# Where the filler matmuls of the projection sit between the steps of four attention heads

## The reference, cut to what matters

```
for l in range(DEPTH):                      # 2
    h = rms_norm(x, norm_mix_pre[l])
    z = h @ w_in[l]                         # one wide projection, split:
    q_h, f_fw, f_bw, i_h, g_h, q_d, k_d, v_d, gate_a, gate_b = split(z)
    a = hgrn2_mixer(q_h, f_fw, f_bw, i_h, g_h, ...)      # 4 heads, both directions
    b = diff_attention(q_d, k_d, v_d, ...)               # 4 heads
    m = sigmoid(gate_a) * (a @ w_branch_a[l]) + sigmoid(gate_b) * (b @ w_branch_b[l])
    x = x + rms_norm(m @ w_out[l], ...)
    x = x + rms_norm(conv_ffn(rms_norm(x, ...), ...), ...)
    x = x + rms_norm(sigmoid(rms_unit(x) @ w_ple_gate[l]) * (p[l] @ w_ple[l]), ...)
```

## The kernel before, in words

| head | 1 | 2 | 3 | 4 | 5 | 6 | 7 | 8 | 10 | 11 | 12 |
|---|---|---|---|---|---|---|---|---|---|---|---|
| second | 20,21 | 22,23 | 24 | 25,26 | 27,28 | 29,30 | 31 | 32 | 33 | 34,35 | 36 |
| third | 37,38 | 39,40 | 41,42 | 43,44 | 45,46 | 47,48 | 49 | 50 | 51,52 | 53 | 54 |
| fourth | 55,56 | 57,58 | 59 | 60,61 | 62,63 | 64,65 | 66 | 67 | 68 | 69,70 | 71 |

## Time and profile before

### The profile page before, as it was taken

One profiled execution on the slowest core, in us unless ns is written; L12 is line 12 of the kernel. 1 busy time (PEld: TensorE's weight loads), 2 busy tenths in 40 slices (PEclk: granted clock), 3 DMA queues, 4 the chain that ended last, 5 costly groups with the idle time before them and its releaser, 6 DMA issues.

```text
span 2431.4 us, 40402 instructions
## 1 busy us (share of the span) xinstructions
PE 2401.2 (99%) x16160; PEld 2235.7 (92%) x16160; DVE 1847.5 (76%) x2432; ACT 1314.8 (54%) x2035; POOL 191.1 (8%) x236
## 2 busy tenths in 40 slices
PE   9999999999999999999999999989999999999998
PEld 8999988898999999888889999888989999998887
DVE  7656887764888998978585578876648889999784
ACT  6445766543555556556454456664435555554563
POOL 1000111100200000003110011101002000000031
PEclk9999999999999999999999999999999999999999
DMA  5354444254323233833234544443543232346421
GB/s 185 127 177 144 134 140 142 99 179 148 104 72 101 83 101 111 297 119 124 97 130 133 182 132 147 137 134 101 180 148 102 75 89 83 105 159 251 150 98 61
DMA packets 287041, 320.97 MB, mean 132 GB/s; under 512 B 10500, under 2 KB 219400, under 8 KB 286856
## 3 DMA queue, kind: packets, MB, share of 16 engines
q1 hardware_dynamic: 213760, 171.39, 22.7%
q10 hardware_dynamic: 73096, 147.01, 16.6%
HBM read 253.08 MB, written 65.27 MB: 131 GB/s over the span
## 4 chain that ended last, share of the span: by engine, by line
PE 93%; DVE 3%; ACT 2%; issue 1%; DMA 0%; SPq 0%; ACTq 0%; DVEq 0%; POOLq 0%; POOL 0%
PE ps L911 23%; PE ps L1196 16%; PE ps L1396 13%; PE ps L1139 7%; PE ps L884 5%; PE ps L1502 5%; PE ps L1365 3%; PE ps L1332 3%; PE ps L898 3%; PE ps L1122 3%; PE ps L1260 3%; PE ps L1111 1%; PE ps L963 1%; PE ps L1091 1%; PE ps L1482 1%; PE ps L1020 1%
## 5 line engine op out<-in xcount | busy, mean ns | idle before, releaser
L2148 DVE TENSOR_TENSOR wlo<-raw,whi 128x1024 fp32r<-128x1024 f32 (+1 forms) x152 | 163.7, 1078 | 55.1 <-ACT whi L3174 55.1
L911 PE MATMUL ps<-hT_hi,whi 128*128 128x384 f32 x608 | 203.1, 334 | 0.0
L911 PE MATMUL ps<-hT_hi,wlo 128*128 128x384 f32 x608 | 203.1, 334 | 0.0
L911 PE MATMUL ps<-hT_lo,whi 128*128 128x384 f32 x608 | 203.1, 334 | 0.0
L3188 ACT ACTIVATE U<-ps 128x384 f32<-128x384 f32 x152 | 74.8, 492 | 223.9 <-PE ps L911 223.9
L1396 PE MATMUL ps<-whi,PH_hi 128*128 128x512 f32 x456 | 179.0, 393 | 0.0
L1396 PE MATMUL ps<-whi,PH_lo 128*128 128x512 f32 x456 | 177.7, 390 | 0.0
L1396 PE MATMUL ps<-wlo,PH_hi 128*128 128x512 f32 x456 | 177.5, 389 | 0.0
L1710 DVE TENSOR_TENSOR wlo<-raw,whi 128x1024 fp32r<-128x1024 f32 (+1 forms) x106 | 111.3, 1070 | 78.9 <-ACT whi L2645 78.8
L1583 DVE TENSOR_TENSOR wlo<-raw,whi 128x2048 fp32r<-128x2048 f32 x51 | 116.6, 2286 | 48.0 <-ACT whi L2469 48.0
L911 PE MATMUL ps<-S_hi,whi 128*128 128x384 f32 x456 | 152.3, 334 | 0.0
(11 more groups left out here) (349 smaller groups left out, 6968.5 us busy)
## 6 DMA issues: line engine op xcount, KB each, us to landing
raw<-w_up_dram SPq DMA_DIRECT2D x88, 512.0 KB
raw<-w_in_dram SPq DMA_DIRECT2D x66, 512.0 KB
raw<-w_down_dram SPq DMA_DIRECT2D x60, 512.0 KB, 4.6
zT<-gst ACTq DMA_DIRECT2D x40, 384.0 KB, 2.4
raw<-w_in_dram SPq DMA_DIRECT2D x14, 1024.0 KB
GT<-zT ACTq DMA_DIRECT2D x16, 768.0 KB, 5.8
zT<-hn ACTq DMA_DIRECT2D x52, 192.0 KB, 1.9
pD<-CG ACTq DMA_DIRECT2D x26, 384.0 KB, 2.3
```

The lines of the kernel that those rows point to most:

```text
L911: ins = mm(ps[:, 4 * (j % 2) + bank, 0:TH], quarter(L, W[y], j, (w,))[:, 0, k * P:(k + 1) * P], sum_operand(a, x, k), start=(opens and k = ...
L2148: v.tensor_tensor(lo, x, hi.bitcast(F32), ALU.subtract)\
```

## The change

Two numbers in the table of slots. The second head's slot 4 gets one part where it had two, and the fourth head's slot 3 gets two where it had one. The sum stays 72.

```diff
-SLOTS = ((2, 2, 2, 2, 2, 2, 2, 1, 1, 0, 2, 1, 1), (0, 2, 2, 1, 2, 2, 2, 1, 1, 0, 1, 2, 1),
-         (0, 2, 2, 2, 2, 2, 2, 1, 1, 0, 2, 1, 1), (0, 2, 2, 1, 2, 2, 2, 1, 1, 0, 1, 2, 1))
+SLOTS = ((2, 2, 2, 2, 2, 2, 2, 1, 1, 0, 2, 1, 1), (0, 2, 2, 1, 1, 2, 2, 1, 1, 0, 1, 2, 1),
+         (0, 2, 2, 2, 2, 2, 2, 1, 1, 0, 2, 1, 1), (0, 2, 2, 2, 2, 2, 2, 1, 1, 0, 1, 2, 1))
```

## The result

The changed kernel takes 2409.35 us (median of 4 runs, 2408.98 to 2409.67) where the kernel before took 2433.8 beside it. The ratio is 0.9901, 95% interval 0.9886 to 0.9916: 24.4 us faster. Forecast were 2409.9. The profiled execution took 2409.67 with a span of 2407.6.

What follows compares the result with a forecast made beforehand. TensorE, busy 2401.2 of 2431.4 us, bounds the kernel; only its waits can be won. Per layer 10.25 + 1.48 + 0.84 - 0.42 - 0.2 = 11.95, for two layers 23.9, giving 2409.9 us, range 2406.5 to 2417.

Steps and rivals of the forecast that it cites:

- The eight copy waits go: TensorE's waits for ScalarE's copy before parts 28 to 56 vanish: 7.85 listed plus 8 x 0.30, 10.25 us a layer.
- The far keys' wait: Third head, before line 1041: the 1.34 us wait goes as part 49 moves to slot 8; gain 1.48 a layer.
- Fourth head, slot 3: A second part there covers an At wait and one for attention weights in level 3; gain 0.84 us a layer.
- Second head, slot 4: Losing its second part, the slot leaves `att_values` waiting for the At copy; cost 0.42 us a layer.
- What gets tight: Part 51's copy and unit 22's low part in the fourth head's level 0 (margin 0.24); 0.2 us a layer together.
- The neighbour: Fourth head's level 0: GpSimd's running products could contend with unit 22's low part; no cost expected, up to 0.6 a layer.
- A: Unit 22's moved halves delay fourth-head weights and third-head x8t copy: 2418.3 us, halfway 2414; chance 0.18 at larger sizes.
- B: ScalarE's queue makes copies late, so each wait returns at the copy's new place: 2430 us; chance 0.05.
- C: Unit 24's load starts later, its lead shrinking from 56.8 to 29.3 us; ScalarE could stall, 2441 at 45 us; chance 0.03.
- D: Second head's slot 4 pays its whole lost cover, 2.05 instead of 0.42 a layer: 2413.2 us; inside the forecast's 0.72.

Runs made afterwards that it cites:

- e1: Against the kernel before: second head's slot 4 gets one part, third head's slot 1 three, so only parts 26 to 36 move; 2429.3 us, ratio 0.9984.
- e2: Against the kernel before: second head unchanged, third head's slot 1 gets one part, from part 38 on everything as in the changed kernel; 2415.14 us, ratio 0.9928.
- e3: Against the changed kernel: third head's slots 1 to 6 hold 1, 2, 2, 2, 2, 3 parts in place of six times 2; 2417.49 us, ratio 0.9935.
- e10: Kernel before with each copy of a gate unit's half cut to its first 384 of 768 columns; 2428.84 us, ratio 0.9982.
- e9: Kernel before with each copy of a gate unit's half preceded by one of its first 384 of 768 columns; 2444.79 us, ratio 1.0049.
- e4: Changed kernel with unit 22's high and low parts made at part 48 (third head's slot 7), not part 49; 2413.06 us, ratio 0.9917.
- e5: Kernel before with every copy of a gate unit's half out of banks 6 and 7 made twice; 2459.28 us, ratio 1.0104.
- e8: Changed kernel with two parts in the second head's slots 3 and 4, one in slot 11, none in slot 12; 2415.18 us, ratio 0.9926.

## Why the prediction was right

**The eight copy waits go, 10.25 a layer.** They went, all sixteen. Idle 15.7 to nothing, and the 0.30 beyond each held: slot 5 lost exactly 5.54 - 4.26. e1 and e2 show it in two parts, e3 puts two back at 0.98 each, and e10 and e9 show that what TensorE stood for was in the main the copy's own length. That ScalarE came late to four of the six copies of one form, by up to 0.6 us, is in the listed idle, so the sum had it without naming it.

**The far keys' wait, 1.48.** It went, and e4 shows by what: with unit 22's two halves one part earlier it is back. There it is worth 1.85 a layer by the medians and 1.74 by the listed waits, more than in the kernel before for the reason told above, so the term was right for the removal.

**Fourth head, slot 3, 0.84.** Both waits are missing from the changed kernel's table. No run took this step alone; it is in e2 and its 18.3.

**Second head, slot 4, -0.42.** One part from 329.28, `att_values` at 331.90: 2.62 against the 2.21 of a part alone, 0.41. The listed wait is 0.29.

**What gets tight, -0.2.** Not spent: neither place has a wait. The rows of the changed kernel, part 51's copy ahead of part 52, and the fourth head's level 1 behind unit 22's low part:

```profile
425.96 0.81 ACT L2598 ACTIVATE hn<-ps 128x768 f32<-128x768 f32 x1 [1.36 <-PE ps L1139]
...
426.97 0.61 PE L1139 MATMUL ps<-hT_hi,whi 128*128 128x384 f32 x2
...
436.30 2.29 DVE L1583 TENSOR_TENSOR wlo<-raw,whi 128x2048 fp32r<-128x2048 f32 x1
...
438.96 0.48 DVE L1842 SCALAR_TENSOR_TENSOR PR<-PR,lr 128x256 f32<-128x256 f32 x1
...
439.69 0.44 PE L1102 MATMUL ps<-ident,PR 128*128 128x128 f32 x2
```

The copy is over at 426.77, 0.20 early, and the weights at 439.44, 0.25 early; I had worked out 0.24. Without the 0.2 the sum is 24.3 for two layers. The heads gained 24.0, the two profiled spans differ by 23.8 and the medians by 24.4, so an agreement closer than some 0.5 us is luck. The neighbour, GpSimd's running products, ends at 435.84, 0.46 before the low part starts, and the low part takes its usual 2.29: no overlap came about, and no run here shows what one would cost.

**The rivals.** A needed the margin in the fourth head to be overrun, or a wait before line 1061 in the third, and there is neither. B, that the copies wait elsewhere, is refuted by ScalarE's waits in the changed kernel: before all 28 copies it is ScalarE that stands, and TensorE's part that it waits for (12 of 28 in the kernel before).

```profile
ACT hn L2598 <- PE ps L1139: 28.1, 14, 2.8
ACT gst L2598 <- PE ps L1139: 15.2, 14, 1.9
```

C, the load of unit 24, started at 438.68 in the changed kernel, 29.1 us before its high part (467.77), as worked out, and nothing waited for it. D would have shown as a long wait in slot 4, where 0.29 is listed. None of the four acted beyond what the sum had. What I had not thought of is the key load of the next head, which came later against the levels; it cost this kernel nothing that its table of waits shows, see the end.

## What to carry to other kernels

Where filler is dealt out in order, its boundaries (an accumulator to be emptied, a unit to be split) move with every count ahead of them. Look at which pieces share a slot before how many there are: here one part moved by two heads took sixteen waits away, and a table with the same counts a head but other pairs gave 8 of the 24 us back, some 5 of them for the pairs. Between a piece that fills an accumulator and the one that needs it again, put other matmuls for at least the copy's length and its ends (here 0.98 us where ScalarE was free for a copy of 0.82, up to 1.54 where it was not), and price such a wait at its listed idle plus 0.3.

## What the runs showed of the hardware that was not expected

TensorE's clock makes the price of a wait uneven. In the kernel before, with sixteen waits of up to 1.54 us before filler parts, and in the changed one no slice of 20 us in the heads has a granted clock below 1.00. With the same waits stretched to between 0.77 and 2.04 (e9) two slices fell to 0.91, with 1.10 to 2.36 (e5) seven, and 25.9 us were lost for 13.3 of idle time. In these two runs the lower level came behind all six waits of 2.04 us and more, behind three of the ten of 1.81 to 1.97, and behind none of the shorter ones. In e8 waits of 0.75 and 1.38, 2.8 us apart, were followed by it in one layer and not in the other. Which property of the idle time decides, these runs don't settle: the single gap's length is not enough, since the clock fell behind 1.38 once and behind 1.54 never.

A transfer became late without anyone moving it. The next head's keys and queries are fetched by SyncE once the last scores of the present head are done; the levels behind it run on TensorE's pace. In the third head VectorE waited 1.13 us for them before, 3.48 in the changed kernel's first layer:

```profile
409.12 1.76 DVE L1818 TENSOR_TENSOR QK<-QK,rope 128x1536 f32<-128x1536 f32 x1 [3.48 <-DMA QKs<-zT]
...
410.80 0.95 DVE L1771 TENSOR_TENSOR QP<-QP,TOT 128x768 f32<-128x768 f32 x1
...
412.44 1.50 PE L1031 MATMUL ps<-QP,KS 128*128 128x128 f32 x12
```

The level 6 update behind it is done at 411.75, 0.69 before line 1031 needs it. Before the change VectorE had stood 3.57 us ahead of this update; now nothing is left of that. 2.4 us went because the load itself took longer, 12.0 us from its issue (397.16) to the product where it had taken 9.6 (403.52 to 413.12), and the rest because TensorE no longer stands before part 48. In the second layer the load took 9.6 where it had taken 9.2, and 1.87 of 3.92 us is left. Why it took 12 us in the first layer is not shown. That margin, and the 0.20 and 0.25 above, are what the next gain in the third head would run into; in e4, with the low part behind the same update, the lateness reached TensorE as 0.42 us.
